# Moving sixteen more tokens out of the dense U product of a PEER layer and fetching their expert rows inside the routing stage

## What is computed

```python
def _peer(h, wq, subkeys, U, V):
    q = (hf @ wq).reshape(T, PEER_HEADS, 2, PEER_HALF)
    s = jnp.einsum('thcd,hcnd->thcn', q, subkeys).astype(jnp.float32)
    sv, si = lax.top_k(s, PEER_TOPK)
    cand = sv[:, :, 0, :, None] + sv[:, :, 1, None, :]
    ...
    fv, fpos = lax.top_k(cand.reshape(T, PEER_HEADS, PEER_TOPK * PEER_TOPK), PEER_TOPK)
    ...
    gates = jax.nn.softmax(fv, axis=-1).astype(h.dtype)
        u = jnp.take(U, ic, axis=0)
        act = jax.nn.gelu(jnp.einsum('chkd,cd->chk', u, xc), approximate=False)
        vv = jnp.take(V, ic, axis=0)
        return jnp.einsum('chk,chkd->cd', gc * act, vv)
```

## Time and profile before

| | |
|---|---|
| median of three runs | 1799.27 us |
| the profiled execution's own time | 1799.91 us |
| its span (first to last instruction) | 1798.2 us |
| mean granted TensorE clock | 0.987 |
| PE busy | 1731.4 us (96%) |
| DVE busy | 1412.4 us (79%) |
| ACT busy | 695.4 us (39%) |
| POOL busy | 603.5 us (34%) |
| HBM traffic over the span | 246 GB/s |

### The profile page before, as it was taken

One profiled execution on the slowest core, in us unless ns is written; L12 is line 12 of the kernel. 1 busy time (PEld: TensorE's weight loads), 2 busy tenths in 40 slices (PEclk: granted clock), 3 DMA queues, 4 the chain that ended last, 5 costly groups with the idle time before them and its releaser, 6 DMA issues.

```text
span 1798.2 us, 36538 instructions
## 1 busy us (share of the span) xinstructions
PE 1731.4 (96%) x12400; PEld 1515.6 (84%) x12400; DVE 1412.4 (79%) x2928; ACT 695.4 (39%) x1304; POOL 603.5 (34%) x481
## 2 busy tenths in 40 slices
PE   5999899889999999899999999999999999999996
PEld 3776788747999999899999999999888888888885
DVE  1885666646878888899999999687698888888877
ACT  3433455514444454433333333334343333333331
POOL 5012633303344353444333343353243332233200
PEclk8999999999999999999999999999999999999998
DMA  9841000254443434699999998999999999999981
GB/s 318 278 155 48 2 3 3 79 202 163 129 135 122 129 123 127 238 321 322 322 327 348 321 317 307 326 411 368 367 412 349 358 351 350 357 357 349 349 281 63
DMA packets 247871, 444.37 MB, mean 247 GB/s; under 512 B 85522, under 2 KB 158580, under 8 KB 247780
## 3 DMA queue, kind: packets, MB, share of 16 engines
q1 hardware_dynamic: 207968, 300.07, 48.0%
q0 software_dynamic: 39168, 142.62, 21.2%
q10 hardware_dynamic: 644, 0.52, 0.2%
HBM read 388.16 MB, written 54.53 MB: 246 GB/s over the span
## 4 chain that ended last, share of the span: by engine, by line
PE 73%; DMA 2%; DVE 1%; SPq 1%; ACT 1%; issue 0%; ACTq 0%; POOL 0%; DVEq 0%
PE bank L1489 26%; PE bank L2030 10%; PE bank L2031 10%; PE bank L2032 10%; PE bank L1469 6%; PE bank L1952 5%; PE bank L2009 4%; PE bank L1427 2%; DMA vsel<-in_peer_v,picks 1%; PE bank L1964 1%; SPq L1460 1%; DMA xrows<-xpicks 0%; DMA uraw<-in_peer_u,xrows 0%; DMA urows<-in_peer_u 0%; DVE n_stats L1393 0%
## 5 line engine op out<-in xcount | busy, mean ns | idle before, releaser
L1489 PE MATMUL bank<-hh,uh 128*128 128x368 f32 x1024 | 350.4, 342 | 0.0
L1489 PE MATMUL bank<-hl,uh 128*128 128x368 f32 x1024 | 337.4, 329 | 0.0
L2030 PE MATMUL bank<-vh,wh 128*128 128x512 f32 x768 | 299.8, 390 | 3.1 <-DVE wl L2443 3.1
L2031 PE MATMUL bank<-vl,wh 128*128 128x512 f32 x768 | 299.6, 390 | 0.0
L2032 PE MATMUL bank<-vh,wl 128*128 128x512 f32 x768 | 299.6, 390 | 0.0
L1547 POOL DMA_INDIRECT vsel<-in_peer_v,picks x128 | 154.2, 1204 | 406.8 <-DVE gt L1573 392.5
L2183 ACT ACTIVATE vh<-vraw 128x1024 fp32r<-128x1024 f32 x128 | 135.9, 1062 | 285.7 <-PE bank L2032 269.6
L1547 POOL DMA_INDIRECT wide<-in_peer_u,picks x108 | 152.6, 1413 | 202.3 <-DVE wide L1554 188.1
L2440 DVE TENSOR_TENSOR vl<-vraw,vh 128x1024 fp32r<-128x1024 f32 x128 | 156.5, 1223 | 80.2 <-ACT vh L2183 80.2
L1489 PEld LDWEIGHTS bank<-hl,uh 128*128 128x128 f32 x1024 | 193.1, 189 | 0.0
L1489 PEld LDWEIGHTS bank<-hh,uh 128*128 128x128 f32 x1024 | 192.8, 188 | 0.0
(11 more groups left out here) (379 smaller groups left out, 2989.1 us busy)
## 6 DMA issues: line engine op xcount, KB each, us to landing
urows<-in_peer_u SPq DMA_DIRECT2D x128, 512.0 KB, 8.2
vraw<-in_peer_v SPq DMA_DIRECT2D x128, 512.0 KB, 6.3
scored<-act_out SPq DMA_DIRECT2D x128, 192.0 KB, 5.2
gates<-SS SPq DMA_DIRECT2D x16, 1536.0 KB, 14.7
gtile<-gates SPq DMA_DIRECT2D x32, 768.0 KB, 7.5
act_in<-scored SPq DMA_DIRECT2D x128, 192.0 KB, 6.3
wt<-in_w_in SPq DMA_DIRECT2D x19, 512.0 KB, 4.4
wq<-in_peer_wq SPq DMA_DIRECT2D x18, 512.0 KB, 3.9
```

Of the source, the lines that this page charges most:

```text
L1489: last = pe.matmul(bank, u[:, k, :], h[:, k, 0:TU], start=(n == 0), stop=(n == 3 * KD - 1))
L2030: pe.matmul(b, wh[s][:, cols], vh[s][:, half], start=first, stop=False)
L2031: pe.matmul(b, wh[s][:, cols], vl[s][:, half], start=False, stop=False)
```

## The change

Sixteen more tokens (`EARLY`, tokens 352 to 367) leave the dense U product, so `TU` is 352 and every matmul of L1489 has 352 columns in place of 368; 352 columns of activations are stored and read back. Their 128 picks per token are laid out as 16 tokens x 8 partition groups, so that one indirect DMA fetches 128 rows, and a head needs two (`PER_HEAD`).

- **DVE** writes a head's picks of these tokens (`ypicks`) at the end of each head. From the second head on, in the middle of head h, it takes two dot products (`row_dot`, 128x1024 each) with the rows of head h - 1, before the second half of the picking.
- **SP** copies `ypicks` into `rows_of` with 8 DMAs of 16x2 elements (`head_picks`). It does this for head i - 1 after the last store of round i, behind a wait on `picked`.
- **POOL** fetches the two row blocks of head i - 1 (`head_rows`) after its last remainder of turn i + 1 in round i, behind a wait on the 8 copies; its next remainder comes after that.
- The last head's two fetches join the 16 extra ones: 18 in the spread turns, two in each of turns 11 to 16 and one in each of 17 to 22. Turn 10 has none, where turn 10 had two before.
- ACT replicates two token tiles at the opening (14 DMAs in place of 7, 4 copies in place of 2); one more small matmul and one more small DVE product close the extra part; DVE fills 32 columns of `act_in` with 1.0 before the V product.

```diff
-TU = TD - EXTRA
-XPAIRS = 2
-XTURNS = EXTRA - XPAIRS
+EARLY = 16
+TU = TD - EXTRA - EARLY
+REPEAT = P // EARLY
+PER_HEAD = TOPK // REPEAT
+LATE_ROWS = PER_HEAD + EXTRA
+XTURNS = 12
+XPAIRS = LATE_ROWS - XTURNS
+FETCHED = HEADS * PER_HEAD + EXTRA
...
+            def head_picks(h):
+                sp.wait_ge(picked, START + h + 1)
+                for b in range(REPEAT):
+                    sp.dma_start(rows_of[EARLY * b:EARLY * (b + 1), bass.ds(PER_HEAD * h, PER_HEAD)],
+                                 ypicks[P - EXTRA - EARLY:P - EXTRA, PER_HEAD * b:PER_HEAD * (b + 1)])\
+                        .then_inc(yrows_in, 16)
...
+            routed(0)
+            with sp.Fori(1, ROUTED) as i:
+                routed(i)
+                head_picks(i - 1)
...
+            def head_rows(h):
...
+                    pool.wait_ge(xdot_up, START + PER_HEAD * h)
+                pool.wait_ge(yrows_in, START + 16 * REPEAT * (h + 1))
+                for k in range(PER_HEAD):
+                    row_fetch(vsel[k], PER_HEAD * h + k, sel.vs_in[k])
+            for i in range(ROUTED - 1):
                 for s in range(4):
                     scores.remainder(pool, i + OPEN, s)
                     if s in (1, 2):
                         query_rest(i + 1, s - 1)
-            with pool.Fori(OPEN + ROUTED - 1, SPREAD) as i:
+                if i:
+                    head_rows(i - 1)
+            for i in range(OPEN + ROUTED - 1, SPREAD):
                 for s in range(4):
                     scores.remainder(pool, i, s)
+                if i == OPEN + ROUTED - 1:
+                    head_rows(HEADS - 2)
...
+                act.wait_ge(hl_up, START + NT)
+                act.activation(hy[0:32, half], banks[4 + j][0:32, :], ACT.Copy).then_inc(ht_out, 1)
+                act.activation(hx[32:48, half], banks[4 + j][32:48, :], ACT.Copy).then_inc(ht_out, 1)
...
+                    if not (first and k == 0):
+                        for f in range(PER_HEAD):
+                            row_dot(vsel[f], sel.vs_in[f], h - 1, hy, PER_HEAD * h + (f - PER_HEAD))
...
-                    dve.sem_inc(picked, 1)
+                    dve.wait_ge(yrows_in, START + 16 * REPEAT * h)
+                    dve.scalar_tensor_tensor(out=ypicks[:, :],
+                                             in0=IS[:, NT - 2, bass.ds(h, 1), :].rearrange("p o k -> p (o k)"),
+                                             scalar=float(NKEYS),
+                                             in1=JS[:, NT - 2, bass.ds(h, 1), :].rearrange("p o k -> p (o k)"),
+                                             op0=ALU.mult, op1=ALU.add).then_inc(picked, 1)
...
+            spread_turn(SPREAD, 0, None)
+            paired = SPREAD + 1 + PER_HEAD // 2
+            for i in range(SPREAD + 1, paired):
+                spread_turn(i, 2, hy)
+            with dve.Fori(paired, SPREAD + 1 + XPAIRS) as i:
+                spread_turn(i, 2, hx)
+            with dve.Fori(SPREAD + 1 + XPAIRS, SPREAD + 1 + XTURNS) as i:
+                spread_turn(i, 1, hx)
```

More of the change, by code:

```diff
@@ L1848, in _, with row_fetch @@
                 query_rest(0, c)
-            with pool.Fori(0, ROUTED - 1) as i:
+            def row_fetch(into, column, landed):
+                pool.indirect_dma_start(out=into[:, :], out_offset=None, in_=sel.rows[0],
+                                        in_offset=bass.IndirectOffsetOnAxis(ap=rows_of[:, column:column + 1], axis=0))\
+                    .then_inc(landed, 16)
+            def head_rows(h):
+                if h == 0:
+                    pool.wait_ge(xrows_in, START + 16 * copies)
+                else:
+                    pool.wait_ge(xdot_up, START + PER_HEAD * h)
[3 more added lines that the diff above has]
+            for i in range(ROUTED - 1):
                 for s in range(4):
@@ L1871, in _ @@
                 fetched(0, 3, 3 * i, 3)
-                for e in range((i < XTURNS) + (i < XPAIRS)):
-                    if i == 0 and e == 0:
-                        pool.wait_ge(xrows_in, START + 16 * (2 * HEADS - 1))
-                        pool.wait_ge(scores.ul_up, START + 4 * SPREAD + 1)
[L1876 to L1881, removed]
+                u = i - 1
+                for e in range((0 <= u < XTURNS) + (0 <= u < XPAIRS)):
+                    if u == 0 and e == 0:
+                        pool.wait_ge(xrows_in, START + 16 * (copies + HEADS))
+                        pool.wait_ge(yrows_in, START + 16 * REPEAT * HEADS)
+                        pool.wait_ge(scores.ul_up, START + 4 * SPREAD + 1)
+                    elif u:
+                        pool.wait_ge(xdot_up, START + PER_HEAD * (HEADS - 1) +
+                                     (2 * (u - 1) + e + 1 if u <= XPAIRS else u + XPAIRS))
+                    q = 2 * u + e if u < XPAIRS else u + XPAIRS
+                    row_fetch(xbuf[e], PER_HEAD * (HEADS - 1) + q, xrow_in[e])
             pool.wait_ge(scores.ul_up, START + 4 * SPREAD + 1)
@@ L2266, in _, with head_pair @@
             dve.wait_ge(iota_up, START + 1)
-            with dve.Fori(0, HEADS // 2) as g:
-                chain.enter(g, 2 * per)
+            def head_pair(g, first):
+                chain.local, chain.loop = 0, (g, 2 * per)
                 step = stepper(dve, chain)
@@ L2461, in group @@
                         sel.add(dve, first + 1, pair + before_v[first + 1], done + 1)
+            for c in range(2):
+                dve.wait_ge(wq_in[c], START + 16 * (HEADS + 1))
+                dve.wait_ge(sk_in[c], START + 16 * (HEADS + 1))
+                dve.wait_ge(sent[c], START + 16 * (BLOCKS // 2))
+            dve.memset(act_in[:, :, TU:TD], 1.0).then_inc(xact_up, 1)
+            dve.wait_ge(xact_up, START + XONES)
             for s in range(4):
```

135 lines of the change are left out of this document (76 added, 59 removed).

## The result

| | before | changed kernel |
|---|---|---|
| median | 1798.65 us (4 runs) | 1830.00 us (4 runs, 1827.94 to 1832.13) |
| ratio, 95% interval | 1 | 1.0179, 1.0167 to 1.0192 |
| profiled execution | 1799.91 us | 1832.13 us |
| PE starts the spread turns | 734.69 us | 773.75 us |
| PE, DVE, POOL busy | 1731.4, 1412.4, 603.5 us | 1726.0, 1457.1, 624.8 us |

A forecast was written before the change was run, and what follows sets the result against it. PE, with 73% of the chain of waits, bounds the kernel; 23.5 - 5.2 + 1.7 - 0.7 - 2.0 - 6.4 - 4.2 = +6.7 us on the profiled 1799.9 gives 1806.6, median 1806; 8-in-10 range 1789 to 1822, forecast's own 1796 to 1817.

The forecast's parts named there:

- the opening: ACT's 14 DMAs end near 456.5, before PE's need at 460.2: cost 0, at the other end 2 us.
- the wait of head 1: Routing: second row block lands 13.3 us into the next round; DVE wants it 1.5 us before that round begins.
- the handing over of heads: Routing after head 1: picks set SP's copies, heads chain at 33.7 us against PE's 32.0, PE held through POOL.
- turn 10: Spread turn without extra rows: PE's 3.46 us wait goes; stage predicted at -4.2 us.
- the end of head 1: Routing: at 549.3 us, 5.2 past its round's end, from 31.0 us of work plus 6.2 of collisions.
- rows 3.6 + 1.8 + 1.2 + 5.7 = 12.3 us after a head's end: Routing ring: eight copies issued 3.6, landing 1.8, second fetch starting 1.2 later, its landing 5.7 us.
- I take one and a half: 33.7 us: Heads 2 to 7: one and a half DVE-POOL collisions (range 2.1 to 6.2 us) on 30.6 us give 33.7.
- Turns 11 to 16: Spread turns with two dots: DVE the bound at 24.5 us each, -2.0 us in all; DMA 0 to 3 us loss.
- Turns 26 to 31: Last spread turns: 24 products with fewer columns save 4.2 us; the V product does not change.
- The rival on the other side: Routing: rows wait but no collisions decide, up to about 2 us per head absorbed; 1789 us, chance 0.17.
- Slower copies: SP's copies: 0.61 us to issue, 3.3 to land, each head 2.1 us longer, +15: 1821 us, chance 0.14.
- The first term: Dense U products: 16 fewer columns save 0.177 us in each of 128, 22.6 us if PE stayed bound.

The follow-up runs named there:

- e9: Changed kernel with DVE's loop over pairs of heads written out: 1824.1 us, ratio 1.0117 to 1.0162 to the kernel before.
- e1: Changed kernel with the two dot products moved from a head's middle to its end, behind the picks: 1808.8 us.
- e2: Changed kernel with POOL fetching the first head's rows for every head and waiting for that head's copies alone: 1831.7 us.
- e8: Kernel before with 352 columns in the dense U product and nothing else, 16 tokens' activations left out: 1781.9 us.
- e6: Changed kernel with SP's copies after the round's first store and the dots at the end of the head: 1783.6 us.
- e7: Changed kernel with dots at the end of the head, late copies, and dots over 16 of 1024 columns: 1788.8 us.
- e10: Changed kernel with early copies, dots ahead of the one-hot products and DVE's loop over head pairs written out: 1787.0 us.
- e13: Changed kernel with SP's copies after the round's first store and nothing else, dots staying in the middle: 1823.0 us.

## Why the prediction came out as it did

- **Right:** the product, 3.84 for 3.82 us; the opening, no wait of PE; SP's copies behind the last store; the wait of head 1; the handing over of heads from then on, with PE held through POOL; the 6.3 us from the last head to PE's spread start, 6.5 predicted; turn 10, -4.5 for -4.2.
- **Right by luck:** the end of head 1, 547.8 for 549.3. Counted from the start of the round, the second dot began at 16.6 us and not at 13.3, while collisions took 3.3 us (one dot, one copy) and not 6.2. The two errors, 3.3 us too little and 2.9 too much, cancel, and the remaining 1.4 us is the round's earlier start.
- **The step that failed** is "rows 3.6 + 1.8 + 1.2 + 5.7 = 12.3 us after a head's end" and "I take one and a half: 33.7 us". Of the 15.6 us by which the routing was predicted too short, all lie in these six heads: 219.6 us for 202.4, less the 1.5 that head 1 ended early. Copies: 5.2 for 3.6, because SP needs 0.65 us a copy; the range's other end (0.61) was nearer. Fetch: 8.7 us for 5.7 in head 5. I had taken the least of three landings since DMA is light in the routing, and did not think of SP, which, waiting for `picked`, holds back its loads and lets them go together with the fetch (the likely cause, not tested alone). In head 5 copies, landing and fetch add 4.4 us up to the second dot, and 2.1 of the predicted 3.1 of collisions come off, since what collides ahead of the second row's arrival costs nothing: 36.1 us for 33.7.
- **Left out altogether:** the 3 us at each of two turns of DVE's loop, of which e9 gave back 3.7 in the heads and 5.9 in the medians, and the remainder that POOL makes behind the fetches. The prediction said that the fetches delay the next `ul`, but not that this puts a POOL subtraction into the stretch where DVE's two-input instructions stood; after that, DVE's own work with its collisions is a second limit (e1, e2).
- **Turns 11 to 16**, predicted at 24.5 us from DVE's busy time, took 25.5. The text had DMA as "0 to 3 us of loss"; the kernel before had one such turn, with its wait, and I reasoned from a turn with one row instead.
- **Turns 26 to 31:** 5.0 of the miss. Some 3.6 of it is turn 27, 24.6 us where the kernel before had 21.7 and 0.7 less was due (PE behind DVE's `ul`). In the other versions of the changed kernel turn 27 took 20.1 to 21.6, so 3 to 4 us of this may belong to that execution, which was also 2.1 us above its median. DVE's row there:

```profile
1207.11 0.69 DVE L1525 TENSOR_TENSOR ul<-bank,uh 128x512 fp32r<-128x512 f32 x1 [2.29 <-issue]
```

- **Rivals.** The rival on the other side put its point of decision at 2 us of collisions per head; they were 3.3 in head 1 and some 4.6 later, and it did not hold. Its sum was off too: with the second dot at 16.6 us head 1 would have ended some 2 us behind the end of its round without any collision, where the rival had it 1.0 ahead. "Slower copies" (1821) was the best of the numbers, though for only half of its reason: the copies issue at 0.65 us each, near its 0.61, but land in 1.9 us, not 3.3. The first term, 22.6 us, measured 18.0 in e8.
- **Open:** why the fetch is longer in the late heads, whether e6 would hold against another phase of POOL and DVE, and the split between DMA and DVE in the turns with two rows.

## What to carry to other kernels

When a helper's result is used inside the loop that makes the next request, add up the whole ring (pick, copy, fetch, use, next pick) and compare it with the round; then move the use behind the next request, and the request to where its data is ready. Where an engine has little slack (little time left over in a round), list every cost that its present wait hides, a loop's turn among them (the narrower kernel of e8 already met it), and look at what each delayed instruction will now stand beside. After taking one limit away and seeing no gain, look for a second one of the same size before giving the first one up.

## What the hardware showed beside this

- A loop's turn on DVE left it idle for 2.8 to 3.4 us in most of the runs where it had nothing to wait for (3.03 and 2.83 in the changed kernel, 3.41 in e7), with more instruction packets on a DMA queue around it than straight code has, and the gap was gone in written-out code (e9, e10). The Trainium skill ("Runtime: NRT & Kernel Launch", Instruction fetch mechanics) says that a taken branch to code outside of what is held forces a fetch before the engine goes on. The trace agrees as far as it goes; the length of the gap is this case's number. Not every turn has it in full: with two dots of 1.2 us ahead of the branch it was 0.67 us (e6).
- A small copy of DVE, with one input, also met POOL: 1.29 us for 0.20 (686.09 above), and in e13 three in a row took 2.3 to 2.4 us each. The Trainium skill ("SBUF — State Buffer", Who interferes with whom) says that `copy`, `cast` and `tensor_scalar` in a mode with two ports contend with POOL as well; the trace agrees. The prediction had counted only instructions with two inputs.
- From the issue of an indirect fetch of 128 rows of 4 KB to DVE's use of them it was 8.7 us in head 5, with the DMA share at 0.90 in 666 to 677 us, and at most 6.3 us in head 1, with 1.04 in 520 to 528 us.
